# Seven-term block products in block 1 and blocks 6 to 11 of the second block's input projections

## The reference, cut to what matters

```python
for l in range(2):
    h = rmsnorm(x, norm_w[l])
    proj = h @ w_in[l]                       # 2048 x 6160
    (ssd_z, ssd_xbc, ssd_dt, cfm_a, cfm_g, cfm_z, att_q, att_k, att_v, att_z) = split(proj)
    y_ssd = ssd_branch(...)                  # causal conv, silu, chunked scan, rmsnorm
    y_cfm = conformer_branch(a, g, z, ...)   # a*sigmoid(g), 31 taps, layernorm, silu
    y_att = diff_attention_branch(...)       # q and k: rmsnorm per head, rope
    x = x + concat([y_ssd, y_cfm, y_att]) @ w_out[l]
```

## Time and profile before

| | |
|---|---|
| median of 3 runs | 3769.35 us (3766.26 to 3773.74) |
| the profiled execution | 3771.97 us, span 3770.2 us |
| PE busy | 3549.1 us (94%) |
| DVE busy | 1626.5 us (43%) |
| ACT busy | 545.8 us (14%) |
| mean granted TensorE clock | 0.961 of full speed |
| L457 (all `column_block` matmuls) | 7232 records, 1724.2 us busy |

### The profile page before, as it was taken

How to read it: one execution, slowest core, us unless ns; L and a number is a source line. 1 busy time by engine, 2 the same in 40 slices (tenths; PEclk the granted TensorE clock), 3 DMA queues, 4 the chain that set the end, 5 groups by cost and what they waited for, 6 DMA issues and landing times.

```text
span 3770.2 us, 49847 instructions
## 1 busy us (share of the span) xinstructions
PE 3549.1 (94%) x21458; PEld 2895.8 (77%) x21458; DVE 1626.5 (43%) x2356; ACT 545.8 (14%) x991; POOL 161.0 (4%) x166
## 2 busy tenths in 40 slices
PE   6999999987899899998999999998999979999979
PEld 2445475546778788887999999997888758888858
DVE  2256942225667610013666667444251251261260
ACT  1000011223434310000100000001011120111120
POOL 0000001000000000000000000000230000230000
PEclk9999999988889999999999999999999989999989
DMA  8878632103322344443444444553343313344303
GB/s 339 316 310 321 256 126 96 56 23 83 78 80 61 92 185 149 178 146 123 162 172 165 168 167 167 181 189 125 133 151 142 110 45 134 132 148 145 112 34 134
DMA packets 134731, 559.12 MB, mean 148 GB/s; under 512 B 57504, under 2 KB 61856, under 8 KB 72112
## 3 DMA queue, kind: packets, MB, share of 16 engines
q1 hardware_dynamic: 120256, 456.17, 34.7%
q10 hardware_dynamic: 14304, 100.42, 6.8%
HBM read 539.24 MB, written 17.30 MB: 148 GB/s over the span
## 4 chain that ended last, share of the span: by engine, by line
PE 68%; DVE 4%; ACT 2%; SPq 1%; DMA 1%; issue 1%; DVEq 0%; ACTq 0%
PE ps L457 36%; PE ps L2444 13%; PE ps L2500 7%; PE ps L1584 2%; PE ps L3096 1%; PE ps L1587 1%; PE ps L1682 1%; SPq L1405 1%; DVE arena L2029 1%; DVE arena L2031 1%; PE ps L2857 0%; DMA pack_t<-arena 0%; SPq L1408 0%; PE ps L3104 0%; PE ps L1461 0%
## 5 line engine op out<-in xcount | busy, mean ns | idle before, releaser
L457 PE MATMUL ps<-arena,ring 128*128 128x256 f32 (+3 forms) x7232 | 1724.2, 401 | 36.3 <-issue 15.7
L457 PEld LDWEIGHTS ps<-arena,ring 128*128 128x128 f32 (+1 forms) x7232 | 1382.7, 191 | 374.7 <-issue 189.7
L2444 PE MATMUL ps<-arena 128*128 128x128 f32 x2560 | 292.4, 275 | 0.0
L2444 PEld LDWEIGHTS ps<-arena 128*128 128x128 f32 x2560 | 289.1, 192 | 0.0
L2444 PE MATMUL ps<-arena,ring 128*128 128x128 f32 x1920 | 220.9, 275 | 0.0
L2444 PEld LDWEIGHTS ps<-arena,ring 128*128 128x128 f32 x1920 | 217.7, 192 | 0.1
L788 DVE SCALAR_TENSOR_TENSOR arena<-arena,small 128x512 f32<-128x512 f32 x240 | 180.5, 752 | 37.0 <-DMA arena<-in_ada_late 20.8
L2500 PE MATMUL ps<-arena 128*128 128x128 f32 x1408 | 161.1, 275 | 0.0
L2500 PEld LDWEIGHTS ps<-arena 128*128 128x128 f32 x1408 | 159.2, 192 | 0.0
L2500 PE MATMUL ps<-arena,ring 128*128 128x128 f32 x1056 | 123.2, 275 | 0.8 <-DVE arena L2597 0.4
L2500 PEld LDWEIGHTS ps<-arena,ring 128*128 128x128 f32 x1056 | 120.2, 192 | 1.7 <-DVE arena L2597 1.7
(11 more groups left out here) (461 smaller groups left out, 3509.5 us busy)
## 6 DMA issues: line engine op xcount, KB each, us to landing
ring<-in_weights SPq DMA_DIRECT2D x402, 1024.0 KB, 4.8
arena<-in_ada_late ACTq DMA_DIRECT2D x64, 1024.0 KB, 8.7
arena<-in_gates SPq DMA_DIRECT2D x56, 256.0 KB, 3.3
arena<-in_front ACTq DMA_DIRECT2D x8, 1024.0 KB, 9.1
arena<-in_x ACTq DMA_DIRECT2D x2, 2048.0 KB, 12.5
keep_g<-arena SPq DMA_DIRECT2D x14, 256.0 KB, 2.0
arena<-keep_h SPq DMA_DIRECT2D x3, 1024.0 KB, 6.2
arena<-in_ctx ACTq DMA_DIRECT2D x1, 2048.0 KB, 23.7
```

Of the source, the lines that this page charges most:

```text
L457: mm = M.matmul(o, ring[:, slot, k, c0:c0 + w], rhs, start=(kc == 0), stop=(kc == ktiles * WK - 1))
L2444: mm = M.matmul(o, w[:, k], x(k), start=(k == 0), stop=(k == HD - 1))
```

## The change

Blocks 1 and 6 to 11 of both later layers become two seven-term pairs each: 14 pairs a layer, numbered k = 0 to 13. Their weight tiles are packed like the feed-forward's (`MIX_SEVEN`). Pair k uses two banks of a half (0 and 1, or 4 and 5), ACT copies the first product (`first_products`), and DVE makes sums (`mix_sums`) and quarters (`mix_quarters`) itself. The small products of blocks 6 to 11 move into banks 2 and 3, or 6 and 7, with a semaphore of their own (`m_small`). DVE's work for blocks 6 to 11 is cut into pieces that stand between the pairs' quarters and sums. PE now waits before block 2 for all quarters of block 1, and before block 6 until ACT has drained blocks 4 and 5.

```diff
-        out += [_tiles(np.concatenate([ca, cg, bc, x, k, q, v, z, cz, az], 1)), _tiles(a['w_out_2'][l])]
+        blocks = np.split(np.concatenate([ca, cg, bc, x, k, q, v, z, cz, az], 1), 12, 1)
+        out += [(_chunk_tiles if n in MIX_SEVEN else _tiles)(w) for n, w in enumerate(blocks)] + [_tiles(a['w_out_2'][l])]
...
+MIX_SEVEN = (1, 6, 7, 8, 9, 10, 11)
...
+        def pair_half(k):
+            return (k + 1) % 2 if k < 2 else k % 2
+        def mix_pair(p, l, k):
+            h, at_tile = pair_half(k), []
...
+            X, Y = ps[:, 4 * h], ps[:, 4 * h + 1]
+            S1, S2, S3, S4 = M_S[h]
+            T1, T2, T3, T4 = M_T
+            A11, A12 = tile()
+            product(X[:, 0:P], A11, lambda n: hB[:, n, 0:P])[0].then_inc(slot_left.sem, slot_left.up(p))
+            product(X[:, P:2 * P], A12, lambda n: hB[:, HD + n, 0:P])
+            A21, A22 = tile()
+            if k == 0:
+                p.wait_ge(m_rows.sem, l + 1)
+            product(Y[:, 3 * P:4 * P], A22, lambda n: T4[:, n])
+            p.wait_ge(m_sums.sem, MPAIRS * l + k + 1)
+            product(Y[:, 0:P], S1, lambda n: T1[:, n])[0].then_inc(slot_left.sem, slot_left.up(p))
+            product(Y[:, P:2 * P], S3, lambda n: T3[:, n])
+            product(X[:, 2 * P:3 * P], S2, lambda n: T2[:, n])
+            product(X[:, 3 * P:4 * P], S4, lambda n: hB[:, HD + n, P:T])[1].then_inc(m_full.sem, 1)
...
+        def mix_sums(v, l, k):
...
+        def mix_quarters(v, l, k):
...
+            def seven(n, extra):
+                base, k = MPAIRS * l, 2 * MIX_SEVEN.index(n)
+                if n == 6:
+                    p.wait_ge(mb.free[0].sem, drained_by(l, 4))
+                    p.wait_ge(mb.free[1].sem, drained_by(l, 5))
+                if n > 7:
+                    p.wait_ge(m_small.sem, 6 * l + n - 7)
+                extra()
+                for i in (k, k + 1):
+                    if n > 6:
+                        p.wait_ge(m_quarters.sem, base + i - 1)
+                    mix_pair(p, l, i)
...
-            column_block(p, mb, 1, 4, lambda kc: hB[:, kc, :],
-                         last_bank=lambda: p.wait_ge(N['dt_in'].sem, N['dt_in'].due(p)))
+            p.wait_ge(mb.free[1].sem, drained_by(l, 1))
+            mix_pair(p, l, 0)
+            p.wait_ge(mb.free[0].sem, drained_by(l, 0))
+            mix_pair(p, l, 1)
+            p.wait_ge(m_quarters.sem, MPAIRS * l + 2)
             block(2)
...
-            block(6, mean)
+            seven(6, mean)
...
-            p.wait_ge(mb.free[0].sem, drained_by(l, 10))
+            p.wait_ge(m_small.sem, 6 * l + 5)
...
+            p.wait_ge(m_quarters.sem, MPAIRS * l + 13)
             xs(0, 0)
-            p.wait_ge(mb.free[1].sem, drained_by(l, 11))
+            p.wait_ge(m_quarters.sem, MPAIRS * l + 14)
+            p.wait_ge(m_small.sem, 6 * l + 6)
...
+            mix_rows(v, l)
+            mix_sums(v, l, 0)
             v.wait_ge(N['dt_mm'].sem, N['dt_mm'].due(v))
...
+            mix_quarters(v, l, 0)
+            mix_quarters(v, l, 1)
             v.wait_ge(N['glu'].sem, N['glu'].due(v))
...
+            mix_sums(v, l, 2)
+            mix_sums(v, l, 3)
+            work = {2: centred, 4: lambda: normed(0), 6: lambda: normed(1), 8: layer_normed,
+                    10: lambda: turned(0), 12: lambda: turned(1)}
+            for k in range(2, MPAIRS):
+                mix_quarters(v, l, k)
+                if k + 2 < MPAIRS:
+                    mix_sums(v, l, k + 2)
+                if k in work:
+                    work[k]()
```

More of the change, by code:

```diff
@@ L2814, in drained_by @@
         def drained_by(l, n):
-            return 1 + 6 * l + n // 2 + 1
+            return 1 + (2 * l + (n - 1) // 2 if n % 2 else 3 * l + n // 2 + 1)
+        MPAIRS = 2 * len(MIX_SEVEN)
+        m_full, m_quarters, m_sums, m_p1, m_rows, m_small = (again(f"mix7_{n}") for n in (
+            "full quarters sums p1 rows small").split())
+        M_T = [view(at, HD, P) for at in (26624, 27648, 28928, 29952)]
+        M_S = [[view(at + 1024 * i, HD, P) for i in range(4)] for at in (36096,)] +\
+            [[view(at, HD, P) for at in (40192, 41216, 42240, 25600)]]
@@ new lines, in build_program, with tile, product @@
+        m_first = view(30976, 2, P)
+        pair_tiles = {}
+        def pair_half(k):
+            return (k + 1) % 2 if k < 2 else k % 2
+        def mix_pair(p, l, k):
+            h, at_tile = pair_half(k), []
+            def tile():
+                slot = take_tile(p)
+                at_tile.append((slot, filled[slot].count['wait', id(p)]))
+                return quadrants(slot)
+            def product(o, w, x):
+                for n in range(HD):
+                    mm = M.matmul(o, w[:, n], x(n), start=(n == 0), stop=(n == HD - 1))
+                    if n == 0:
+                        first = mm
+                return first, mm
+            X, Y = ps[:, 4 * h], ps[:, 4 * h + 1]
[13 more added lines that the diff above has]
+            product(X[:, 3 * P:4 * P], S4, lambda n: hB[:, HD + n, P:T])[1].then_inc(m_full.sem, 1)
+            pair_tiles[l, k] = at_tile
@@ new lines, in mix_rows @@
+        def mix_rows(v, l):
+            v.wait_ge(nb["hb"].sem, nb["hb"].due(v, 4))
+            B11, B12, B21, B22 = (hB[:, HD * k:HD * k + HD, P * t:P * t + P] for k in range(2) for t in range(2))
+            T1, T2, T3, T4 = M_T
+            V.tensor_tensor(T1, B12, B11, ALU.subtract).then_inc(dve_step.sem, dve_step.up(v))
+            V.tensor_tensor(T3, B22, B12, ALU.subtract).then_inc(dve_step.sem, dve_step.up(v))
+            v.wait_ge(dve_step.sem, dve_step.now(v))
+            V.tensor_tensor(T2, B22, T1, ALU.subtract).then_inc(dve_step.sem, dve_step.up(v))
+            v.wait_ge(dve_step.sem, dve_step.now(v))
+            V.tensor_tensor(T4, B21, T2, ALU.subtract).then_inc(m_rows.sem, 1)
@@ L2837, in sums @@
                 for c in range(4):
-                    M.matmul(second(bank), C('ones'), src[:, c], start=(c == 0), stop=(c == 3))
+                    M.matmul(ps[:, bank, 0:T], C('ones'), src[:, c], start=(c == 0), stop=(c == 3))
             def mean():
@@ L2908, in chunk4, with first_products, small_in, projected @@
                 return pj[:, 4 * n:4 * n + 4]
+            def first_products(*ks):
+                for k in ks:
+                    a.wait_ge(m_full.sem, MPAIRS * l + k + 1)
+                    S.copy(m_first[:, pair_half(k)], ps[:, 4 * pair_half(k), 0:P]).then_inc(m_p1.sem, 1)
+            def small_in(dst, bank):
+                src = ps[:, bank, 0:T] if len(dst.shape) == 2 else\
+                    ps[:, bank:bank + 2, :].rearrange("p b (c t) -> p b c t", c=2)
+                to = dst if len(dst.shape) == 2 else dst.rearrange("p (b c) t -> p b c t", c=2)
+                S.copy(to, src).then_inc(m_small.sem, 1)
+            def projected(n):
+                a.wait_ge(m_quarters.sem, MPAIRS * l + 2 * MIX_SEVEN.index(n) + 2)
             def root(line_in, x, line_out):
@@ L2955, in mix_act @@
             a.wait_ge(act_step.sem, act_step.now(a))
+            projected(11)
             silu(44, 4)
@@ L3032, in mix_dve, with small, centred, normed @@
                     v.wait_ge(ready.sem, ready.now(v))
[L3034 to L3039, removed]
+            def small(n):
+                v.wait_ge(m_small.sem, 6 * l + n - 5)
+            def centred():
+                small(6)
+                V.scalar_tensor_tensor(cx[:], over(mean_c, 4, T), -1.0 / 512, cc[:], ALU.mult, ALU.add)\
+                    .then_inc(lx['centred'].sem, lx['centred'].up(v))
+                v.wait_ge(lx['centred'].sem, lx['centred'].now(v))
+            def normed(half):
                 x, m = qk[:, 4 * half:4 * half + 4], sqa[:, 4 * half:4 * half + 4]
-                block = 7 + half
-                v.wait_ge(mb.free[block % 2].sem, drained_by(l, block))
+                small(7 + half)
                 V.tensor_scalar(m, m, 1.0 / 64, EPS, ALU.mult, ALU.add).then_inc(at['ms_in'].sem, at['ms_in'].up(v))
@@ L3047, in mix_dve, with layer_normed, turned @@
                 v.wait_ge(dve_step.sem, dve_step.now(v))
-                V.scalar_tensor_tensor(x, x, K2(l, norm), m, ALU.mult, ALU.mult)\
+                V.scalar_tensor_tensor(x, x, K2(l, ('kn_w', 'qn_w')[half]), m, ALU.mult, ALU.mult)\
                     .then_inc(at['normed'].sem, at['normed'].up(v))
                 v.wait_ge(at['normed'].sem, at['normed'].now(v))
[L3051 to L3061, removed]
+            def layer_normed():
+                small(9)
+                V.tensor_scalar(rs_c, rs_c, 1.0 / 512, EPS, ALU.mult, ALU.add)\
+                    .then_inc(lx['var_in'].sem, lx['var_in'].up(v))
+                v.wait_ge(lx['var_in'].sem, lx['var_in'].now(v))
+                v.wait_ge(lx['root'].sem, lx['root'].due(v))
+                V.reciprocal(rs_c, rs_c).then_inc(dve_step.sem, dve_step.up(v))
+                v.wait_ge(dve_step.sem, dve_step.now(v))
```

(6 more changed lines are left out.)

70 lines of the change are left out of this document (55 added, 15 removed).

## The result

The changed kernel takes 3736.72 us (median of 4 runs, 3729.70 to 3743.34) against 3771.55 us for the kernel before in all its runs by then: a ratio of 0.9906, 95% interval 0.9881 to 0.9931. The forecast was 3735, range 3728 to 3752. One of the ten executions of the kernel with sums one pair ahead took 5156.56 us, at a mean granted clock of 0.661, and is left out of its ratio.

A forecast was written before the change was run, and what follows sets the result against it. PE was taken to bound the input projections. A layer: -18.3 us (pairs) + 2.38 + 1.54 (waits before blocks 2 and 6) - 3.36 (stage end) = -17.7; two layers with the clock -34.0, giving 3735 us, range 3728 to 3752.

The forecast's parts named there:

- The pair: In the input projections, a seven-term pair takes 12.51 us against half a block's 13.82, saving 18.3 us a layer.
- rival 4: Pairs, unrolled and beside a busier DVE, take half a block's 13.8 us and save nothing: 3770 us; chance 0.05.
- DVE's room: In blocks 6 to 11 PE never waits for DVE; quarters 5 end 4.3 us before pair 7 needs them.
- Rival 3: DVE is late behind the norms in blocks 7 and 8, at four places: 3759 us; chance 0.07.
- Rival 5: Sums come late in every pair, PE waits 5.05 us in each of 28 pairs: 3876 us; chance 0.06.
- The wait before block 2: Before block 2 PE waits for the quarters of pair 1, adding 2.38 us a layer that nothing hides.
- Before block 6: Before block 6 PE waits for ACT's copy of block 5, adding 1.54 us a layer.
- The end: Between block 11 and the scan, 10.11 us become 6.75 as the rotation runs under pair 13: 3.36 us less a layer.
- The clock: Behind the new waits, one fall of PE's clock in the two layers, at 1.45 us.
- rival 2: The clock falls at all four new gaps, before blocks 2 and 6 in both layers: 3740 to 3750 us; chance 0.12.
- The sum: Pairs, two waits and stage end together: 17.7 us less a layer, 35.4 in two, 34.0 with the clock.
- DVE's busy time: Over the whole kernel, the added sums and quarters raise DVE's busy time by about 195 us.

The follow-up runs named there:

- sums one pair ahead: Against the changed kernel, DVE makes the sums of pair k+1, not k+2, behind the quarters of pair k; 3771.06 us, 0.9986 of the kernel before.
- 64-column run: Against the changed kernel, every product of the pairs takes 64 of its 128 moving columns; 3788.32 us (one run).
- longer norms: Against the changed kernel, the reciprocal in the norms of k and q is taken three times in place of once; 3778.74 us.
- late wait: Against the changed kernel, the wait for block 5's drain stands before pair 3 in place of before block 6's small product; 3733.39 us.
- last rotation: Against the changed kernel, the last rotation stands behind the quarters of pair 13 in place of pair 12; 3747.67 us.
- the repeat: The changed kernel again, unchanged, to compare on one chip; 3737.07 us.

## Why the prediction was right

**The pair.** 25.01 / 2 = 12.51 us, as read from the feed-forward part, at a clock of 1.00. The unrolled code and the busier DVE changed nothing, so rival 4 falls. Why 12.51 and not less, the 64-column run and the rows in the last section show: a load of 128 weight columns takes as long. The `column_block` line has 7232 - 5440 = 1792 records fewer, as forecast.

**DVE's room.** 4.3 us was forecast at pair 7 and 5.0 found, 4.7 and 5.5 for the sums. The longer norms confirm it by their waits. Rival 3's mechanism is real, as the longer norms show, but it did not come in by itself. Rival 5 was right that the lead is what counts, and its case didn't arise; one pair less of lead cost 16 us a layer.

**The wait before block 2.** Forecast 2.38 of idle PE; the hole is 2.09 (2.11 in the timeline), just under the 2.2 to 2.4 named as a sign, and 0.26 of slower restart, for which the sum had no term, makes it 2.35. So the mechanism was right and the agreement of the price is partly luck. **Before block 6:** forecast 1.54; 2818.76 - 2815.60 = 3.16 less the small products' 1.73 is 1.43. Here too the chain's idle time is less than the price, 1.19. **The end:** forecast 6.75 to the scan, measured 6.72, with quarters 13, the `cb` products, the masks and the scaling in the order forecast.

**The clock.** One fall in two layers was taken at 1.45 us; there was one, at 29.58 - 27.89 = 1.69. That it was one was luck in part: over this run and five experiments that kept the wait and the full columns (late wait, one ahead, longer norms, last rotation, and the repeat), block 2 took 29.58 in two cases and 27.89 in the other ten, with the same gap of 2.11 us each time. So rival 2, a fall at all four gaps, did not come, and behind the wait before block 6 none was seen. The two that fell stand behind the shortest block 1 of the twelve, 26.44 and 26.41 us against 26.56 to 27.95; why was not tried.

**The sum.** Without the fall a layer was to give 17.7 us; the second gave 17.95 and the first 16.13, which is 17.8 with the fall's 1.69 taken out (the sign of 17 to 18 us held in the second layer alone). The two stages together gave 34.1 us against the 34.0 summed, and the medians differ by 34.8. DVE's busy time rose by 1813.0 - 1626.5 = 186.5 us against some 195 forecast: partly because the four operations of the quarters are busy for 3 x 0.42 + 0.29 = 1.55 us and not 1.65; the rest is not accounted for.

## What to carry to other kernels

A cheaper product on the bounding engine is worth its difference times its count, provided that the work it needs from another engine is queued far enough ahead: the same DVE work one pair later took back 30.6 of 34.1 us. A block that needs a wait of its own must earn that wait first; block 1 did not, until its banks were chosen so that the next block could start without waiting for its quarters (345.02 us against 347.77 with block 1 in full tiles). And an order of small pieces at a stage's end can be a good part of what a change seems to bring: here 3.2 of the second layer's 17.95 us.

## What the runs showed of the hardware

With 128 moving columns or 64, a float32 matmul of a 128x128 weight that changes each time takes the same: 111.7 and 111.4 ns a record at full clock, while 256 columns take 215.9. It is not a fixed cost of a record, as rows of the changed kernel show:

```profile
949.90 0.34 PE L1695 MATMUL ps<-arena 128*64 128x64 f32 x4
...
951.97 1.20 PE L1511 MATMUL ps<-con,arena 128*128 128x128 f32 x9
...
2989.29 0.22 PE ps L3258 x2
```

Between the first two rows, of the timeline, lie 64 records of 64 weight columns by 64 moving columns: 32 ns apart at a granted clock of 1.00 (they write to the two halves of the partitions in turn and may overlap; two at a time would be 64 ns each). So for 64 moving columns it is the 128 weight columns that hold a record at 111.4. The third row, of the chain, has 64 weight columns and 128 moving ones, and takes 110 ns a record: at 128 by 128 both sides take about the same. The Trainium skill (TensorE: Matmul & The Clock Gate, "LDWEIGHTS (loading the stationary operand)") has the load grow with the weight's columns alone; an estimate by its rule is 106.7 ns for 128 of them. These rows agree in kind and lie 5 ns above.

Behind the narrow time-step products the clock is low, though PE is busy without a pause through them. Windows of the changed kernel at their start (2664.56) and near their end:

```profile
2665.00:2668.00 3.00, 3.00 (x29) 3.00 (x28) 0.00 (x0) 2.05 (x2) 0.00 (x0) 1.00 0.00 0
...
2670.00:2673.00 3.00, 3.00 (x16) 3.00 (x15) 0.00 (x0) 0.00 (x0) 0.00 (x0) 0.50 0.00 0
```

How long it stays low varied from run to run: block 1 took between 26.41 and 27.95 us for the same instructions, 1.4 to 2.9 us over the 25.01 of the later blocks. With products of only 64 columns there it stayed at 0.50 through all of block 1, to 2726, and came back in the 256-column block 2. The same 64-column products did not lower it in blocks 6 to 11, where it was 1.00 when they began. What decides this was not tried.

By gap: behind 1.19 us before block 6, and behind the sixteen of 1.59 to 1.77 us with sums one pair ahead, the matmuls ran on at full pace; behind 2.11 us before block 2 the clock fell in 2 of 12 cases; behind the four of 6.92 to 8.05 us it was low each time.
